# Scan of a two-block network: projections cut into eight pieces, some placed ahead of the corrections, and one step's scores placed one level earlier

## The reference, cut to what matters

```python
def step(S, inp):
    r_t, k_t, v_t, d_t, kk_t, a_t = inp
    s_kk = jnp.einsum('bhvk,bhk->bhv', S, kk_t)
    S_new = (S * d_t[:, :, None, :]
             - s_kk[..., None] * (kk_t * a_t)[:, :, None, :]
             + v_t[..., None] * k_t[:, :, None, :])
    y = jnp.einsum('bhvk,bhk->bhv', S if reverse else S_new, r_t)
```

## Time and profile before

| what | us |
|---|---|
| median of three runs | 3378.59 |
| lowest and highest | 3375.62, 3390.28 |
| the profiled execution, measured | 3390.49 |
| its span | 3388.8 |
| TensorE busy | 2934.9 (87%) |
| VectorE busy | 1159.6 (34%) |
| ScalarE busy | 640.9 (19%) |
| GpSimd busy | 254.2 (8%) |

### The profile page before, as it was taken

The page is one execution under the profiler, slowest core; times in us unless marked ns, Lnnn a source line. Parts: engine busy times, 40 slices in busy tenths (PEclk is TensorE's granted clock), DMA queues, the critical chain, the costliest instruction groups (busy, mean ns, idle before and its releaser), DMA issues. The chain is left out here.

```text
span 3388.8 us, 69285 instructions
## 1 busy us (share of the span) xinstructions
PE 2934.9 (87%) x30694; PEld 1639.7 (48%) x30694; DVE 1159.6 (34%) x2595; ACT 640.9 (19%) x1430; POOL 254.2 (8%) x291
## 2 busy tenths in 40 slices
PE   5799999999987999977888988898857886899987
PEld 3477677767774444444332333333323444345543
DVE  3345554555453662152011012102032334223332
ACT  1233333333331010000000000000001343022221
POOL 1111211121110000000000000000000121010000
PEclk9899999999998999988999999999988997899988
DMA  4100000000004772235999999999943111122212
GB/s 160 42 17 18 16 24 18 18 17 23 4 5 172 261 277 86 107 127 219 426 431 430 428 425 428 426 422 429 430 206 100 39 40 49 30 58 56 56 28 81
DMA packets 192362, 561.66 MB, mean 166 GB/s; under 512 B 32476, under 2 KB 120050, under 8 KB 167510
## 3 DMA queue, kind: packets, MB, share of 16 engines
q1 hardware_dynamic: 192054, 557.45, 42.5%
q10 hardware_dynamic: 32, 0.03, 0.0%
HBM read 554.84 MB, written 2.27 MB: 164 GB/s over the span
## 5 line engine op out<-in xcount | busy, mean ns | idle before, releaser
L2119 PE MATMUL bank<-ex_ring,xe 128*64 128x512 f32 x2048 | 471.3, 614 | 101.2 <-DMA ex_ring<-in_exp_w_dram 95.7
L2119 PEld LDWEIGHTS bank<-ex_ring,xe 128*64 128x64 f32 x2048 | 169.4, 141 | 400.7 <-issue 390.0
L2119 PE MATMUL bank<-ex_ring,hidT 128*64 128x512 f32 x1024 | 226.9, 598 | 7.0 <-DMA ex_ring<-in_exp_w_dram 6.5
L2291 DVE TENSOR_TENSOR ex_acc<-ex_acc,bank 128x512 f32<-128x512 f32 x64 | 44.0, 688 | 515.9 <-PE bank L2155 515.9
L712 PE MATMUL bank<-hT,wj 128*128 128x512 f32 x384 | 203.1, 658 | 5.6 <-DVE vj L1498 2.9
L3022 PE MATMUL bank<-h2T_mixer,na_w 128*128 128x512 f32 x384 | 183.8, 628 | 18.8 <-DMA na_w<-in_odd_w_in_dram 18.8
L2599 PE MATMUL bank<-h2T_mixer,ev_w 128*128 128x512 f32 x320 | 155.7, 639 | 29.4 <-DMA ev_w<-in_even_w_in_dram 21.3
L1766 PE MATMUL bank<-hT,mg_ring 128*128 128x512 f32 x384 | 169.1, 599 | 1.5 <-PE bank L1766 1.5
L2119 PEld LDWEIGHTS bank<-ex_ring,hidT 128*64 128x64 f32 x1024 | 73.2, 138 | 142.6 <-issue 139.5
L1437 DVE TENSOR_TENSOR pm<-bank,m_level 128x512 f32<-128x512 f32 x120 | 82.7, 689 | 159.4 <-PE bank L806 158.5
L876 PE MATMUL bank<-pm,XT 64*64 64x32 f32 x3072 | 107.1, 220 | 27.4 <-DVE pm L1437 27.1
(11 more groups left out here) (480 smaller groups left out, 4898.0 us busy)
## 6 DMA issues: line engine op xcount, KB each, us to landing
ex_ring<-in_exp_w_dram SPq DMA_DIRECT2D x192, 2048.0 KB, 18.4
ws_w<-in_ada_w_dram SPq DMA_DIRECT2D x40, 1024.0 KB, 5.3
mg_ring<-in_w_in_dram SPq DMA_DIRECT2D x8, 2048.0 KB, 8.9
na_w<-in_odd_w_in_dram SPq DMA_DIRECT2D x32, 512.0 KB, 6.1
wj<-in_w_in_dram SPq DMA_DIRECT2D x24, 512.0 KB, 4.0
ev_w<-in_even_w_in_dram SPq DMA_DIRECT2D x24, 512.0 KB, 7.0
ada_ring<-in_ada_w_dram SPq DMA_DIRECT2D x4, 2048.0 KB, 19.8
mg_ring<-in_w_branch_a_dram SPq DMA_DIRECT2D x2, 2048.0 KB, 7.7
```

The costliest lines, as they stand in the source:

```text
L2119: r[e] = mm(out[a, :], lhs[j][:, a], w[:, j, 512 * c:512 * c + 512], start=(first and j == 0), stop=(last and j == len(lhs) - 1), skip_gro ...
L2291: dve.tensor_tensor(acc[:, n, c], acc[:, n, c], bank[6 + o % 2][:], ALU.add).then_inc(S["added"], 1)
```

## The change

`project` is cut into eight pieces instead of four: one 128x512 matmul per piece for K_X, R_X and V_X, two 128x256 matmuls for K_V. A helper calls several pieces in a row. What moves in TensorE's order: two matmuls of K_X now stand in slot (0, 0, 0), ahead of `solve` and `correct`, and one fewer in each of (0, 0, 1) and (0, 1, 1); one matmul of R_X stands in (1, 4, 0), ahead of `correct_last`, instead of (1, 4, 1); `scores(j, 8)` stands in (1, 1, 1) instead of (1, 2, 0). K_V and V_X are called in more pieces in the same slots. The order of the other engines is the same.

```diff
                 if which == K_V:
-                    i, o = (1, PROJ[:, 0:TC]) if piece < 2 else (2, PROJ[:, TC:2 * TC])
-                    for c in range(4 * (piece % 2), 4 * (piece % 2) + 4):
+                    i, o = (1, PROJ[:, 0:TC]) if piece < 4 else (2, PROJ[:, TC:2 * TC])
+                    for c in range(2 * (piece % 4), 2 * (piece % 4) + 2):
                         last = mm(o, wj[:, c, i, :], hT[:, c, T:TA], start=(c == 0), stop=(c == KT - 1))
                 else:
                     i = {K_X: 1, R_X: 0, V_X: 2}[which]
-                    for c in range(2 * piece, 2 * piece + 2):
-                        last = mm(PROJ[:], wj[:, c, i, :], hT[:, c, 0:T], start=(c == 0), stop=(c == KT - 1))
-                if piece == 3:
+                    last = mm(PROJ[:], wj[:, piece, i, :], hT[:, piece, 0:T], start=(piece == 0), stop=(piece == KT - 1))
+                if piece == 7:
                     last.then_inc(S["proj"], 1)
+
+            def pieces(j, which, lo, hi):
+                for piece in range(lo, hi):
+                    project(j, which, piece)
...
                 if at == (0, 0, 0):
                     turn_params(b)
+                    pieces(b, K_X, 0, 2)
                 if at == (0, 0, 1):
-                    project(b, K_X, 0)
+                    pieces(b, K_X, 2, 3)
                 if at == (0, 1, 0):
-                    project(b, K_X, 1)
+                    pieces(b, K_X, 3, 5)
                     bonus(j)
                 if at == (0, 1, 1):
-                    project(b, K_X, 2)
+                    pieces(b, K_X, 5, 6)
                 if at == (0, 2, 0):
-                    project(b, K_X, 3)
+                    pieces(b, K_X, 6, 8)
                     scores(j, 4)
...
+                if at == (1, 1, 1):
+                    scores(j, 8)
                 if at == (1, 2, 0):
-                    scores(j, 8)
                     scores(j, 9)
...
                 if at == (1, 3, 0):
-                    project(b, R_X, 0)
+                    pieces(b, R_X, 0, 2)
                     squares(b)
                 if at == (1, 3, 1):
-                    project(b, R_X, 1)
+                    pieces(b, R_X, 2, 4)
+                if at == (1, 4, 0):
+                    pieces(b, R_X, 4, 5)
                 if at == (1, 4, 1):
-                    project(b, R_X, 2)
+                    pieces(b, R_X, 5, 6)
                 if at == (2, 0, 0):
-                    project(b, R_X, 3)
+                    pieces(b, R_X, 6, 8)
                     spread_inverse(b)
...
```

More of the change, by code:

```diff
@@ L1025, in beside @@
                     decays(b, 2)
-                    project(b, K_V, 0)
+                    pieces(b, K_V, 0, 2)
                 if at == (1, 0, 0):
                     variance(a)
-                    project(b, K_V, 1)
+                    pieces(b, K_V, 2, 4)
                 if at == (1, 0, 1):
-                    project(b, K_V, 2)
+                    pieces(b, K_V, 4, 6)
                 if at == (1, 1, 0):
-                    project(b, K_V, 3)
+                    pieces(b, K_V, 6, 8)
                     spread_rstd(a)
                     gate(a)
+                if at == (1, 1, 1):
+                    scores(j, 8)
                 if at == (1, 2, 0):
-                    scores(j, 8)
                     scores(j, 9)
@@ L1065, in beside @@
                     cumulate(b, 5)
-                    project(b, V_X, 0)
+                    pieces(b, V_X, 0, 2)
                 if at == (2, 3, 1):
-                    project(b, V_X, 1)
+                    pieces(b, V_X, 2, 4)
                 if at == (2, 4, 0):
-                    project(b, V_X, 2)
+                    pieces(b, V_X, 4, 6)
                 if at == (2, 4, 1):
-                    project(b, V_X, 3)
+                    pieces(b, V_X, 6, 8)
             BESIDE = {(0, 0): ("V", 0), (1, 0): ("V", 1), (1, 1): ("B", 1), (1, 2): ("K", 1), (1, 3): ("V", 2), (1, 4): ("B", 2),
```

## The result

Ten executions each: 3361.35 us after (3350.31 to 3375.04) against 3379.19 us before (3375.62 to 3390.28), ratio 0.9942 with a 95% interval of 0.9924 to 0.996. The kernel is faster by 0.6%, 17.8 us by the medians; 3357 was forecast, 21.9 us less. The changed kernel scatters over 25 us, the one before over 15.

The account below looks back on a forecast made before the run. TensorE was taken to set the scan's time. Gains of 12.0, 5.2, 0.7 and 9.9 us less 5.9 lost made 21.9 us, taking the median from 3378.6 to about 3357 us; range 3345 to 3374.

Parts of the forecast that it names:

- rival (2): Clock gain gone entirely: (1,2) falls every turn, or (0,0) falls as before; 3361 to 3362 us; chance 0.17.
- D: Level (0,0): filling the idle time there restores the full clock; 8.2 us in five turns plus 1.7 in turn 0, 9.9.
- A: K_X matmuls into (0,0,0): insertion costs 0, removals from (0,0,1) and (0,1,1) gain 1.72 us per turn, 12.0 in all.
- B: R_X matmul from (1,4,1) to (1,4,0): delays the last correction about 0.10, gains net 0.75 us per turn, 5.2 in all.
- C: scores(8) from (1,2,0) to (1,1,1): hole only moved, 0 gained in turns 0 to 6, 0.7 us in turn 7.
- E: Level (1,2): the unbroken 1.83 us hole lowers the clock in 3.6 of six turns, 1.65 us each, 5.9 us lost.
- The sentence that nothing is given back: Stages behind the scan start as much earlier and have no clock of their own to meet; 0 us lost there.

## Why the prediction was right, and where it wasn't

The direction, the time and the main mechanism held: 3361.35 against 3357, within the range. That the time came so close is in part luck, and the median alone doesn't pick the forecast: rival (2) gave 3361 to 3362. The profiles do. Level (0,0) is at full clock in every one of turns 1 to 6, and (1,2) fell in some turns only; turns 0 to 6 gained 22.4 to 26.0 us in the four profiles that have the whole change there, where the forecast's terms give 21.2 and rival (2) 17.2. Of this gain 17.8 us are left in the medians, so a term that was too pessimistic and a loss that wasn't foreseen partly cancel. The profiles of turns 0 to 6 can be set in a row that isolates each term, since each differs from the one above by one edit. Each is one execution, and two of the same turns differ by up to 3.6 us:

| kernel | turns 0 to 6, us | step | measured | predicted |
|---|---|---|---|---|
| before | 780.81 | | | |
| two spare matmuls in (0,0) | 769.77 | D, clock at (0,0) | 11.0 | 9.9 |
| K_X alone | 757.94 | A, moved matmuls | 11.8 | 12.0 |
| K_X and R_X, two profiles | 753.49, 754.86 | B | 4.5, 3.1 | 5.2 |
| the change, four profiles | 755.10, 758.41, 755.58, 754.83 | C and E | -1.8 by the means | 0, -5.9 |

*A.* Right to 0.2 us, and so was its cover: `correct` follows the mask by 0.05 us behind two projections and `solve`. ScalarE's copy of U, put at some 0.3 us, took 0.28. No product waited longer for XT than before.

*B.* 0.65 us a turn by the length of level (1,4), instead of 0.75: the last correction starts 2.15 us behind the level's first product, where it was 1.95, so the insertion cost 0.20 and not the 0.10 I allowed. The removal was worth 0.85, where 0.86 was put.

*C.* Right: the mask of (1,2) starts when the shifts end (0.03 us behind the last, before and after), wherever the product stands. Turn 7's level (1,2) is 5.24 us after and 5.94 before, the 0.7 that was booked.

*D.* Right, and shown without moving anything. In five of turns 1 to 6 of the kernel before, level (0,0) took 9.45 to 9.72 us at 0.82 to 0.85, each with a stretch at 0.50 in it, and in turn 5 it took 8.07 at 1.00; the two spare matmuls made it 8.06 or 8.07 in all six. Turns 1, 3, 4 and 6 of before, then a stretch of turn 2, stand here beside the earlier trace rows:

```profile
273.96:283.67 9.71, 7.36 (x174) 4.68 (x174) 6.22 (x13) 1.35 (x4) 1.13 (x1) 0.82 0.22 58
...
498.84:508.54 9.70, 7.34 (x174) 4.45 (x173) 6.22 (x13) 1.35 (x4) 1.13 (x1) 0.83 0.20 57
611.23:620.68 9.45, 7.10 (x174) 4.39 (x173) 6.22 (x13) 1.34 (x4) 1.13 (x1) 0.85 0.21 58
...
834.34:844.00 9.66, 7.30 (x174) 5.09 (x173) 6.22 (x13) 1.35 (x4) 1.13 (x1) 0.82 0.20 58
...
392.55:395.96 3.41, 3.41 (x8) 1.17 (x4) 1.35 (x5) 0.00 (x0) 0.00 (x0) 0.50 0.03 7
```

Of the prediction's choices this was the one least to be taken for granted; the row that gave it was one level at two clocks in the same execution. Turns 1 to 6 gave 7.5 us where 8.2 was put. Turn 0, for which I took half of 3.4, gave 3.5: there the clock came back in full, from 0.97 over the turn to 1.00.

*E.* The low clock came where I put it, but at too high a price. In the five profiles with the moved scores, scores(8) alone included, one, three, one, one and one of six turns fell: 7 of 30, where 3.6 of six were assumed. In the seven profiles with the scores in their old place none of 42 did. By the means of the turns above it cost 1.8 us and not 5.9, though single profiles differ by more than that. One unbroken hole of 1.74 us here was followed by the low clock less often than 0.50 and 1.86 close together (five of six before); I treated them as nearly equal. The 3.6 was my estimate from how near the two holes are, and what length of hole lowers the clock isn't shown: both kinds were followed by it in some turns and not in others.

*The sentence that nothing is given back.* As an assumption this failed. I took everything from turn 7 on as a constant, because no instruction of it changed but scores(8). Its instructions didn't change, its clock can: in turn 7 no next pair is projected, TensorE waits up to 0.7 us in front of most `solve`s and many products (ten times, 6.5 us, and eight times, 4.1 us, from turn 7 on in the first profile), and it can lie at the low clock for tens of microseconds. In the first profile that cost 8.6 us of the 25.7, in the second of the same program 1.7; over the profiles, turn 7 to the merge takes 111.8 to 126.3 us in the eight without spare work there, and 110.6 to 110.7 in the three with all of it. It was my term of nothing that was wrong; its true size isn't shown.

What stays open is whether the changed kernel falls into the low clock there more often than the one before. The whole runs hint at it: the spare work is worth 9 to 11 us on one and 2 to 3 on the other, with intervals that overlap. The profiles don't: without spare work in turn 7, the four kernels with K_X moved take 111.8, 119.4, 123.9 and 126.3 us, and the four without it 117.7, 118.0, 120.3 and 123.6. The moved scores aren't needed for it (123.9 us in a profile without them), and filling the first hole of turn 7 alone didn't prevent it. No experiment fills only the holes around the place where the long stretches begin, nor shifts where turn 7 begins. That a low stretch keeps itself up, as I put it for the spare work in turn 7, isn't shown either.

The fastest version is the change with spare matmuls in turns 7 and 8: 0.9913 of before, 3349.08 us, and 0.9914 with the scores in their old place.

## What to carry to other kernels

Where an engine that sets the time waits for another at a fixed place of a loop, move work of its own from behind the wait to in front of it, and check in the other engine's timeline that the waited-for instruction is late for its own reasons; here each moved matmul of K_X was then worth its full length (11.8 us for fourteen, 0.84 each, where 0.86 was put), and one more entry in a hole whose end is set elsewhere was worth nothing (level (1,2) of turn 2 kept its 7.26 us). Look for a low granted clock just behind the hole: here its return was worth about as much as the moved work (11.0 and 11.8 us), and spare matmuls into a free bank told the two apart. Don't take the last turn of a pipelined loop as a constant when it does less than the others: here its time lay anywhere from 111.8 to 126.3 us by the clock, with nearly the same instructions. And take several profiles of a kernel before a term of 2 or 3 us is read from one.

## What the runs showed of the hardware that was not expected

Extra work made the kernel faster twice: 14 matmuls of 128x512 in holes gave 11 us (0.9967), 22 of 128x256 in the last turns some 9 to 11 us of the changed kernel (0.9944 to 0.9913, two neighbouring intervals). In turn 7 the low clock held for 47.75 us while TensorE was 38.61 us busy in it (1006 matmul records; those of the product on px took 313 ns on average), where the kernel before was 41.08 us busy in 50 us of the same turn, with 1596 records (233 ns for the same product), and kept 0.97. And code that no edit touches differs from profile to profile: over the twelve of this case, what lies ahead of the scan took 159.9 to 167.1 us and what lies behind it 2317.4 to 2324.9. So the clock of turn 7 is one part of the 25 us over which the ten runs of the change spread, and not shown to be all of it.
